# First stage in eight conditioning groups of two feature tiles instead of four of four, and background conditioning blocks at other places

## The chip, the cores and the metric

One NeuronCore of a Trainium2 chip. The metric is the device time of one execution in microseconds. The engines are TensorE (PE), ScalarE (ACT), VectorE (DVE), GpSimd (POOL, which only issues DMAs here) and SyncE (SP, DMAs too).

## The reference

One layer of a diffusion backbone: 512 latent tokens and 256 context tokens of 2048 features, all in float32. What matters here:

```python
sh1, sc1, gt1, sh2, sc2, gt2 = modulation(c, w_ada, b_ada)          # silu(c) @ w_ada + b_ada, 2048 -> 12288
csh1, csc1, ...              = modulation(c_ctx, w_ada, b_ada)      # only shift and scale 1 are used
hc = modulate(rms_norm(ctx, g_mix_pre), csh1, csc1)                 # h * (1 + scale) + shift
hx = modulate(rms_norm(x,   g_mix_pre), sh1,  sc1)
u_f, u_x, u_g = split(h @ w_in)    # Fourier group, RG-LRU input, RG-LRU gate branch; 1024 features each
# x_c = conv(u_x); bidirectional RG-LRU on ctx, then on x; times gelu(u_g); Fourier mix of u_f
x = x + gt1 * rms_norm(concat(...) @ w_out, g_mix_post)
x = x + gt2 * rms_norm(conv_ffn(modulate(rms_norm(x, g_ffn_pre), sh2, sc2)), g_ffn_post)
```

## The kernel before, in words

Features lie on the partitions: x is 16 feature tiles of 128 x 512, ctx 16 of 128 x 256. Every float32 product is three matmuls (`three`, L679 on): a rounded high part and a low part of weights and of activations, hi*hi, hi*lo, lo*hi. The weights come as a stream of units of 128 x 1024 (eight 128 x 128 blocks, 512 KB) through a ring of five slots. SP loads unit n when unit n - 5 has been used (`load_unit`), ACT rounds it (`hi`, L377), DVE takes the difference (`lo`, L1013), and PE uses the blocks. Each engine runs a list of instructions whose order is written out by hand, with semaphores between them.

**The conditioning.** `w_ada` has 12288 columns. The first 4096 (shift and scale 1) are needed before anything can be projected. They are computed on PE in the first stage, for c and c_ctx at once: `ada_unit` (L694) multiplies a loaded unit of 128 x 1024 (one row tile k, 512 columns of shift and 512 of scale) by the two columns of csil, into two of the four 32-column strips of the array, so that units of even and odd k run beside each other. After 16 units a group of four feature tiles has its sums as rows in bank 5; ACT copies them (`copy_rows`, L406), and PE turns them into columns in bank 7 (`turn`, L706, with `pick`, which also adds the strips up).

**The first stage** (L688 to L750). PE adds up the squares of x and of ctx with ones-matmuls. Then, for each of four groups: DVE's `modulate` (L1101) makes gains, scales the tiles of x and ctx, ACT's `round_h` (L412) makes the high parts, DVE the low parts (L1121, L1123), and PE's `first_heads(k)` (L721) multiplies tile k with the weights of heads 0 and 1: the gate branch (u_g) and the input (u_x, also for ctx). The units of the next group go between the tiles. All sums of heads 0 and 1 are complete only with tile 15, since the tiles are summed over k.

**The heads.** For h in 0 to 7 PE projects head h + 2 and computes the recurrence gates of head h; ACT does the seeds of the convolution (`seeds`), gelu, sigmoids, exponentials and roots; DVE convolves, combines and scans (`convolve`, `gap`, `finish_head`). In heads 6 and 7 PE turns to the Fourier projections.

**The Fourier stage** (four groups: weights_dft, channel_mix, token_dft), with halves of the output projection between, then **the output projection**: tiles 4 to 15 each take two weight units, and DVE adds the square of each tile (`add_square`), splits the weights of the tile after the next, adds positions to the residual (`place`), and eats background blocks. Then the norms, and the feed-forward part.

**The background blocks.** The other 8192 columns of `w_ada` are 8 sums of 16 blocks each, 128 x 1024, 512 KB. POOL loads them into three slots (`load_ada`, L333): block q is loaded when q - 2 are eaten. DVE eats a block (`eat_ada`, L1034): acc = acc + block * csil, one instruction of 128 x 1024. After 16 blocks PE sums acc over the partitions (`sum_ada`, L759: 8 matmuls of one column), and DVE reads the result (`take_ada`, L1056). There are two accumulators; a sum's first block waits until the sum that had its accumulator is done (`ADA_FREE`). How many blocks each head eats is in `ADA_SLOT`, after which output tile a sum is made in `SUM_AFTER`, and in which round of DVE it is taken in `TAKE_AT`. Before the output projection 32 blocks have been eaten, in it 64, in the feed-forward part 32.

Of the kernel before, what the change touches and what calls it, by code (L numbers as in the profile page):

```python
# [13 lines left out]
P = 128  # L14
# [18 lines left out]
UX, UG = {0: (1, 7), 1: (1, 7)}, {0: (0, 6), 1: (0, 6)}  # L33
# [31 lines left out]
NADA = 4  # L65
# [3 lines left out]
NBG = (6 * D - NADA * 1024) // ACOL  # L69
FFN_ADA = NBG - 2  # L70
ADA_SLOT = (4, 3, 3, 3, 3, 0, 3, 3)
ADA_FREE = (0, 1, 0, 2, 3, 4, 6, 7)
SUM_AFTER = {4: 1, 6: 2, 9: 3, 12: 4, 15: 5}
TAKE_AT = {5: 1, 7: 2, 10: 3, 13: 4}
# [35 lines left out]
def build(nc, x_t, ctx_t, par_d, late_d, stream, ada0, adabg, gates_d, tabs_d, wf_d, out_t):  # L110
    ctx = ExitStack()
    with ctx:
# [44 lines left out]
        with ExitStack() as s:  # L157
            c0, hc_lo = twice(s, "c0", "hc_lo", [P, KT, C])
            hc_hi = sbuf(s, "hc_hi", [P, KT, C], F32R)
            with ExitStack() as s0:  # L160
                sq0 = sbuf(s0, "sq0", [P, 2, L])
                ss_x = sbuf(s0, "ss_x", [P, L])
                ss_c = sbuf(s0, "ss_c", [P, C])
                pos0 = sbuf(s0, "pos0", [P, NPOS])
                ada_rows = sbuf(s0, "ada_rows", [P, 512])
                ada0_raw = sbuf(s0, "ada0_raw", [P, A0SLOTS, 1024])
# [56 lines left out]
        def ada_acc(n):  # L223
            return (ada_acc1 if n in (2, 4) else ada_acc0)[:, :]
# [4 lines left out]
        x_in, c_in = [sem(f"x_in{i}") for i in range(4)], sem("c_in")  # L229
# [11 lines left out]
        h_pre, h_rounded, h_ready = sem("h_pre"), sem("h_rounded"), sem("h_ready")  # L241
        gates_done, xc_seed, xc_done, xc_round, xc_split = (
# [48 lines left out]
        def _(sp):  # L291
# [12 lines left out]
            for i in range(4):  # L304
                sp.dma_start(x0[:, 4 * i:4 * i + 4, :], x_t[:, 4 * i:4 * i + 4, :]).then_inc(x_in[i], 16)
                load_a0(i)
            for i in range(2):
                sp.dma_start(c0[:, 8 * i:8 * i + 8, :], ctx_t[:, 8 * i:8 * i + 8, :]).then_inc(c_in, 16)
# [22 lines left out]
        def _(pool):  # L331
# [23 lines left out]
            load_ada(19, 25)  # L355
# [4 lines left out]
            load_ada(25, 30)  # L360
            load_wf(2)
            load_ada(30, 32)
            load_wf(3)
            load_ada(32, 34)
            pool.wait_ge(yc_ready, KT)
            pool.dma_start(late_par[:, :], late_d).then_inc(late_in, 16)
            for j in range(4):
                pool.dma_start(x1[:, 4 * j:4 * j + 4, :], x_t[:, 4 * j:4 * j + 4, :]).then_inc(x1_in[j], 16)
                load_ada(34 + 8 * j, 42 + 8 * j)
            load_ada(66, NBG * KT)  # L370

        @block.scalar
        def _(act):
# [24 lines left out]
            act.wait_ge(c_in, 32)  # L398
            for k in range(KT):
                square(sq0[:, k % 2, 0:C], c0[:, k, :], KT + k)  # L400
            act.wait_ge(csil_done, 2)
            act.wait_ge(sq_added, 2 * KT)
            std(bank[0], ss_x[:, :])
            std(bank[1], ss_c[:, :])

            def copy_rows(c):  # L406
                act.wait_ge(a0_used, KT * c + KT)
                if c > 0:
                    act.wait_ge(turned, c)
                a.activation(ada_rows[:, :], bank[5][:, :], ACT.Copy).then_inc(rows_copied, 1)  # L410

            def round_h(c):  # L412
                for k in range(4 * c, 4 * c + 4):
# [5 lines left out]
            hi(0, 1)  # L419
            copy_rows(0)  # L420
            round_h(0)
            hi(2, 3)
            copy_rows(1)
            round_h(1)
            hi(4)
            copy_rows(2)
            round_h(2)
            hi(5)
            copy_rows(3)
            hi(6, 7)  # L430
            round_h(3)
            hi(8, 9)

            def gelu(h):
                act.wait_ge(*used(UG[h][1]))
# [46 lines left out]

            seeds(0)
            hi(10, 11)
            gelu(0)
            gelu(1)
# [189 lines left out]
        def _(pe):  # L676
# [17 lines left out]
            def ada_unit(u):  # L694

                k, s = u % KT, u % A0SLOTS
                pe.wait_ge(a0_in[s], 16 * (u // A0SLOTS) + 16)
                if k == 0 and u > 0:
                    pe.wait_ge(rows_copied, u // KT)
                for part in range(2):  # L700
                    g = 32 * (2 * (k % 2) + part)
                    mm = t.matmul(bank[5][g:g + 2, :], csil[:, 2 * k:2 * k + 2], ada0_raw[:, s, 512 * part:512 * part + 512],  # L702
                                  start=k < 2, stop=k >= KT - 2, tile_position=(0, g))
                mm.then_inc(a0_used, 1)

            def turn(c):  # L706
# [3 lines left out]
                for j in range(4):  # L710
# [3 lines left out]
            for k in range(KT):  # L714
                ada_unit(k)
                pe.wait_ge(sq_done, KT + k + 1)
                mm = t.matmul(bank[1][:, 0:C], ones, sq0[:, k % 2, 0:C], start=k == 0, stop=k == KT - 1)
                mm.then_inc(sq_added, 1)
            pe.wait_ge(std_done, 2)

            def first_heads(k):  # L721

                c, j = k // 4, k % 4
                g_unit, x_unit = 2 * c, 2 * c + 1
                pe.wait_ge(h_ready, k + 1)
                if j == 0:
                    pe.wait_ge(lo_done, g_unit + 1)
                for h in range(2):
                    mm = three(bank[UG_BANK[h]][:, :], *block_of(g_unit, 4 * h + j), h_hi[:, k, :], h_lo[:, k, :], k == 0, k == KT - 1)
                if j == 3:  # L730
                    mm.then_inc(unit_used, 1)
                if j == 0:
                    pe.wait_ge(lo_done, x_unit + 1)
                for h in range(2):
                    bx, bc = ux_bank(h)
                    w, w_l = block_of(x_unit, 4 * h + j)
                    three(bx[:, :], w, w_l, h_hi[:, k, :], h_lo[:, k, :], k == 0, k == KT - 1)
                    mm = three(bc[:, 0:C], w, w_l, hc_hi[:, k, :], hc_lo[:, k, :], k == 0, k == KT - 1)
                if j == 3:
                    mm.then_inc(unit_used, 1)  # L740

            for c in range(NADA):
                for j in range(4):
                    if c + 1 < NADA:
                        for u in range(KT * (c + 1) + 4 * j, KT * (c + 1) + 4 * j + 4):
                            ada_unit(u)
                    if j == 0:
                        turn(c)
                    first_heads(4 * c + j)
# [9 lines left out]
            def sum_ada(n, b):  # L759
# [805 lines left out]
```

## Time and profile before

| | us |
|---|---|
| median of 3 runs (lowest, highest) | 2279.06 (2275.04, 2281.58) |
| the profiled execution | 2278.63 |
| its span | 2276.8 |
| busy: PE, DVE, ACT | 2146.7, 1219.5, 715.8 |
| mean granted clock of PE | 0.969 |

The profile is one execution. The page gives the busy share of each engine in 40 slices of the span (57 us each) in tenths, and the clock that PE was granted. A list of waits says how long an engine stood and what ended it. A timeline lists instructions in order of time, with the idle time ahead of them in brackets. A window row gives the busy time of each engine in a stretch. Matmul durations include the way through the array, so the distance between starts is what a matmul costs in a row of them.

### The profile page before, as it was taken

How to read it: one execution, taken by the hardware profiler on the slowest of the kernel's cores; microseconds unless marked ns; L12 is line 12 of the kernel's file. 1: busy time of each engine (PE TensorE's matmuls, PEld its weight loads, DVE VectorE, ACT ScalarE, POOL GpSimd, SP SyncE). 2: the span in 40 equal slices, each digit the busy share in tenths (PEclk: the TensorE clock that was granted, in tenths of full speed). 3: DMA queues.
4: the chain of work that ended last, by engine and by line, in shares of the span. 5: the costliest groups of instructions: out<-in, count | busy, mean ns of one | idle time of the engine just before them, and what ended most of it. 6: DMA issues, size and time to landing. Idle time of an engine off the chain costs nothing.

```text
span 2276.8 us, 23135 instructions
## 1 busy us (share of the span) xinstructions
PE 2146.7 (94%) x9668; PEld 1725.2 (76%) x9668; DVE 1219.5 (54%) x1491; ACT 715.8 (31%) x926; POOL 74.8 (3%) x145
## 2 busy tenths in 40 slices
PE   7779999999788699999999999999999999999994
PEld 2457888888667388888888888888888888888883
DVE  2545887885666865454454544434344443434447
ACT  3224667543122333222222322222232222222222
POOL 0000000010211000000000000000000000000000
PEclk9889999999888799999999999999999999999997
DMA  9743433343777134343333432232232322232321
GB/s 387 271 182 111 130 114 114 132 159 111 285 251 260 44 133 136 119 140 102 122 128 129 133 108 93 93 100 95 93 102 93 95 100 93 94 100 93 97 98 74
DMA packets 83192, 302.39 MB, mean 133 GB/s; under 512 B 9296, under 2 KB 9424, under 8 KB 81808
## 3 DMA queue, kind: packets, MB, share of 16 engines
q1 hardware_dynamic: 63360, 227.03, 29.1%
q0 software_dynamic: 19728, 73.89, 9.7%
q8 instruction: 76, 1.25, 0.2%
q14 instruction: 28, 0.23, 0.0%
HBM read 296.69 MB, written 4.19 MB: 132 GB/s over the span
## 4 chain that ended last, share of the span: by engine, by line
PE 69%; DVE 7%; DMA 3%; ACT 1%; issue 1%; DVEq 0%; ACTq 0%
PE bank L681 23%; PE bank L683 23%; PE bank L682 23%; DMA ada_raw<-in_adabg 2%; DVE ada_acc L1053 2%; DVE w_lo L1017 1%; PE bank L762 1%; DVE x L1379 0%; DVE x L1452 0%; DVE acc L1377 0%; DVE acc L1450 0%; DVE ss L1029 0%; ACT w_hi L380 0%; DMA w_raw<-in_stream 0%; DVE x L1356 0%
## 5 line engine op out<-in xcount | busy, mean ns | idle before, releaser
L681 PE MATMUL bank<-h_hi,w_hi 128*128 128x512 f32 x2048 | 809.4, 395 | 34.6 <-DVE hc_lo L1123 15.9
L682 PE MATMUL bank<-h_lo,w_hi 128*128 128x512 f32 x2048 | 804.9, 393 | 0.0
L683 PE MATMUL bank<-h_hi,w_lo 128*128 128x512 f32 x2048 | 803.4, 392 | 0.0
L1017 DVE TENSOR_TENSOR w_lo<-w_raw,w_hi 128x1024 fp32r<-128x1024 f32 x344 | 411.3, 1222 | 636.5 <-ACT w_hi L380 636.3
L380 ACT ACTIVATE w_hi<-w_raw 128x1024 fp32r<-128x1024 f32 x344 | 353.0, 1056 | 1097.3 <-PE bank L683 1034.5
L681 PEld LDWEIGHTS bank<-h_hi,w_hi 128*128 128x128 f32 x2048 | 389.5, 190 | 120.4 <-DVE hc_lo L1123 16.3
L683 PEld LDWEIGHTS bank<-h_hi,w_lo 128*128 128x128 f32 x2048 | 388.9, 190 | 82.8
L682 PEld LDWEIGHTS bank<-h_lo,w_hi 128*128 128x128 f32 x2048 | 389.7, 190 | 75.5
L683 PE MATMUL bank<-act_hi,w_lo 128*128 128x512 f32 x704 | 278.1, 395 | 0.0
L681 PE MATMUL bank<-act_hi,w_hi 128*128 128x512 f32 x704 | 278.0, 395 | 0.0
L682 PE MATMUL bank<-act_lo,w_hi 128*128 128x512 f32 x704 | 278.0, 395 | 0.0
L1427 DVE TENSOR_TENSOR acc<-acc,bank 128x512 f32<-128x512 f32 x160 | 109.1, 687 | 173.9 <-PE bank L683 173.9
L1053 DVE SCALAR_TENSOR_TENSOR ada_acc<-ada_raw,csil,ada_acc 128x1024 f32<-128x1024 f32 x120 | 153.8, 1281 | 45.2 <-DMA ada_raw<-in_adabg 40.8
L682 PEld LDWEIGHTS bank<-act_lo,w_hi 128*128 128x128 f32 x704 | 132.1, 188 | 32.1
L683 PEld LDWEIGHTS bank<-act_hi,w_lo 128*128 128x128 f32 x704 | 132.1, 188 | 32.1
L681 PEld LDWEIGHTS bank<-act_hi,w_hi 128*128 128x128 f32 x704 | 132.1, 188 | 32.0
L342 POOL DMA_DIRECT2D ada_raw<-in_adabg x128 | 67.7, 529 | 1191.4 <-DVE ada_acc L1053 803.1
L604 ACT ACTIVATE acc<-bank 128x512 f32<-128x512 f32 x16 | 9.5, 596 | 147.1 <-PE bank L683 147.1
L762 PE MATMUL bank<-par,ada_acc 128*128 128x1 f32 x128 | 21.4, 297 | 35.8 <-DVE ada_acc L1053 35.8
L762 PEld LDWEIGHTS bank<-par,ada_acc 128*128 128x128 f32 x128 | 21.4, 258 | 37.7 <-DVE ada_acc L1053 37.5
L702 PE MATMUL bank<-ada_raw,csil 128*2 128x512 f32 x256 | 41.7, 634 | 4.9 <-ACT ada_rows L410 4.9
L682 PE MATMUL bank<-hc_lo,w_hi 128*128 128x256 f32 x128 | 36.5, 285 | 0.0
(188 smaller groups left out, 1468.3 us busy)
## 6 DMA issues: line engine op xcount, KB each, us to landing
w_raw<-in_stream SPq DMA_DIRECT2D x344, 512.0 KB, 3.5
ada_raw<-in_adabg POOLq DMA_DIRECT2D x128, 512.0 KB, 4.6
ada_raw<-in_ada SPq DMA_DIRECT2D x64, 512.0 KB, 7.0
x<-in_x_t SPq DMA_DIRECT2D x4, 1024.0 KB, 12.2
x<-in_x_t POOLq DMA_DIRECT2D x4, 1024.0 KB, 6.9
out_t<-x SPq DMA_DIRECT2D x16, 256.0 KB, 2.0
c<-in_ctx_t SPq DMA_DIRECT2D x2, 1024.0 KB, 18.7
g_raw<-in_gates SPq DMA_DIRECT2D x8, 256.0 KB, 4.2
```

Source lines behind the costliest of these rows:

```text
L342: pool.dma_start(ada_raw(s), adabg[q]).then_inc(ada_in[s], 16)
L380: a.activation(w_hi[:, n % RING, :], w_raw[:, n % RING, :], ACT.Copy).then_inc(hi_done, 1)
L604: a.activation(tile(acc, m), b[:, :], ACT.Copy).then_inc(y_copied, 1)
L681: t.matmul(out, w, v, start=start, stop=False)
L682: t.matmul(out, w, v_l, start=False, stop=False)
L683: return t.matmul(out, w_l, v, start=False, stop=stop)
L702: mm = t.matmul(bank[5][g:g + 2, :], csil[:, 2 * k:2 * k + 2], ada0_raw[:, s, 512 * part:512 * part + 512], start=k < 2, stop=k >= KT - 2, ...
L762: mm = t.matmul(b[:, j:j + 1], ada_acc(n)[:, P * j:P * j + P], ones[:, 0:1], start=True, stop=True)
L1017: v.tensor_tensor(w_lo[:, s, :], w_raw[:, s, :], w_hi[:, s, :].bitcast(F32), ALU.subtract).then_inc(lo_done, 1)
L1053: v.scalar_tensor_tensor(dst, ada_raw(s), scale, dst, ALU.mult, ALU.add).then_inc(ada_eaten, 1)
L1427: v.tensor_tensor(tile(acc, m), tile(acc, m), bank[4 + m % 4][:, :], ALU.add).then_inc(down_added, 1)
```

## The change

- The first 4096 columns come in eight groups of two feature tiles (NADA 8). A unit now holds two row tiles k and, of each, 256 columns of shift and 256 of scale; 8 units make a group, 64 in all as before. `ada_unit` issues four matmuls of 256 columns into the four strips.
- SP loads x and ctx ahead of all conditioning units, and weight unit c behind the fourth unit of group c. Weight units 0 to 7 each hold the gate and the input weights of heads 0 and 1 for two tiles.
- PE adds up the squares of ctx first, then runs the 8 units of group 0. ACT makes the root for x after the fourth square of ctx.
- In each group PE runs the first unit of the next group, the turn, four more units, gates of tile 2c, inputs, two units, gates and inputs of tile 2c + 1, the last unit. In the last group both gates come ahead of the inputs, and ACT's gelu of heads 0 and 1 waits for the gates alone (`first_ug`), ahead of its seeds.
- Background blocks: heads eat 28 instead of 22, the Fourier stage 12 instead of 10, the output projection 56 instead of 64. The sum of blocks 0 to 15 is made in head 4 (bank 4), that of 16 to 31 in `channel_mix(2)` (bank 6, columns 8 to 15), the sums 2 to 5 after output tiles 6, 9, 13 and 15.

```diff
-ADA_SLOT = (4, 3, 3, 3, 3, 0, 3, 3)
-SUM_AFTER = {4: 1, 6: 2, 9: 3, 12: 4, 15: 5}
+ADA_SLOT = (4, 4, 4, 4, 0, 4, 4, 4)
+SUM_AFTER = {6: 2, 9: 3, 13: 4, 15: 5}
@@ sync
-                load_a0(i)
...
-            for u in range(4, NADA * KT):
+            for u in range(NADA * A0UNITS):
                 load_a0(u)
-                at = {8: (0, 1), 24: (2, 3), 30: (4,), 46: (5,), 60: (6, 7)}
-                for n in at.get(u, ()):
-                    load_unit(n)
+                if u % A0UNITS == 3:
+                    load_unit(u // A0UNITS)
@@ scalar
             for k in range(KT):
+                if k % 8 == 0:
+                    act.wait_ge(c_in[k // 8], 16)
                 square(sq0[:, k % 2, 0:C], c0[:, k, :], KT + k)
+                if k == 3:
+                    std(bank[0], ss_x[:, :])
...
+            hi(0)
+            for c in range(NADA):
+                copy_rows(c)
+                round_h(c)
+                hi(c + 1)
...
+            gelu(0)
+            gelu(1)
+            hi(9)
             seeds(0)
             hi(10, 11)
-            gelu(0)
-            gelu(1)
@@ tensor
+                for q in range(4):
+                    k, g = 2 * i + q // 2, 32 * q
+                    mm = t.matmul(bank[5][g:g + 2, 0:2 * P], csil[:, 2 * k:2 * k + 2], ada0_raw[:, slot, 256 * q:256 * q + 256],
+                                  start=i == 0, stop=i == A0UNITS - 1, tile_position=(0, g))
...
             for c in range(NADA):
+                after = range(A0UNITS * (c + 1), A0UNITS * (c + 2)) if c + 1 < NADA else ()
+                for u in after[0:1]:
+                    ada_unit(u)
+                turn(c)
+                for u in after[1:5]:
+                    ada_unit(u)
+                pe.wait_ge(lo_done, c + 1)
+                pe.wait_ge(h_ready, 2 * c + 1)
+                gates_of_two(2 * c)
+                if c + 1 < NADA:
+                    inputs_of_two(2 * c)
+                    for u in after[5:7]:
+                        ada_unit(u)
+                    pe.wait_ge(h_ready, 2 * c + 2)
+                    gates_of_two(2 * c + 1)
+                    inputs_of_two(2 * c + 1)
+                    for u in after[7:8]:
+                        ada_unit(u)
+                else:
+                    pe.wait_ge(h_ready, 2 * c + 2)
+                    gates_of_two(2 * c + 1)
+                    inputs_of_two(2 * c)
+                    inputs_of_two(2 * c + 1)
...
                 project_gate(h + 2)
+                if h == 4:
+                    pe.wait_ge(xc_done, 6)
+                    sum_ada(0, bank[4])
                 gates(h, 1)
+                if h == 4:
+                    pe.wait_ge(ada_read, 1)
             pe.wait_ge(xc_done, 7)
-            sum_ada(0, bank[2])
...
                 mm.then_inc(nyq_done, 1)
+                if g == 2:
+                    sum_ada(1, bank[M_BANK[0]], 8)
@@ vector (Fourier stage)
-            eat_ada(3)
+            eat_ada(2)
...
-            eat_ada(2)
+            eat_ada(1)
...
             split_yc(8, 9)
-            eat_ada(2)
...
             split_yc(10, 11)
-            eat_ada(1)
+            take_ada(1, bank[M_BANK[0]], 8)
...
             fourier_input(7)
+            eat_ada(2)
             lo(56)
             fourier_output(2)
+            eat_ada(1)
             split_yc(12, 13)
             read_nyq(3)
             split_p(3)
-            eat_ada(1)
+            eat_ada(2)
             fourier_output(3)
             split_yc(14, 15)
+            eat_ada(3)
@@ vector (output projection, in round m)
                 if 3 <= m < 15:
-                    eat_ada(6 if m % 3 == 0 else 5)
+                    eat_ada(4 if m % 3 == 2 else 5)
```

## Rows read from the trace of the kernel before

**Rows 1.** The page, 40 slices: busy tenths of PE and its granted clock.

```profile
PE   7779999999788699999999999999999999999994
...
PEclk9889999999888799999999999999999999999997
```

**Rows 2.** Windows: stretch, length, busy us of PE, PEld, DVE, ACT, POOL, PEclk, DMA share, GB/s.

```profile
0.00:57.00 57.00, 42.66 (x128) 12.02 (x128) 12.52 (x24) 21.17 (x39) 0.20 (x4) 1.00 0.98 387
57.00:182.00 125.00, 97.05 (x514) 63.74 (x515) 56.25 (x97) 35.85 (x55) 1.71 (x3) 0.85 0.58 216
```

**Rows 3.** Waits of PE over the span: total us, times, longest.

```profile
PE bank L762 <- DVE ada_acc L1053: 35.8, 4, 13.4
PE bank L681 <- DVE hc_lo L1123: 15.9, 4, 4.0
...
PE bank L681 <- DVE w_lo L1017: 4.3, 2, 3.5
```

**Rows 4.** Timeline of PE, first stage: start, us, instruction, count, idle before.

```profile
12.81 17.27 PE L691 MATMUL bank<-sq,par 128*128 128x512 f32 x32 [12.81 <-ACT sq L385]
...
30.98 0.70 PE L717 MATMUL bank<-sq,par 128*128 128x256 f32 x2
...
81.43 1.90 PE L702 MATMUL bank<-ada_raw,csil 128*2 128x512 f32 x16
83.26 0.50 PE L681 MATMUL bank<-h_hi,w_hi 128*128 128x512 f32 x1
...
86.93 1.90 PE L702 MATMUL bank<-ada_raw,csil 128*2 128x512 f32 x16
...
99.28 0.80 PE L681 MATMUL bank<-h_hi,w_hi 128*128 128x512 f32 x1 [3.98 <-DVE hc_lo L1123]
...
122.75 1.05 PE L711 MATMUL bank<-par,ada_rows 128*128 128x4 f32 x8
127.78 0.80 PE L681 MATMUL bank<-h_hi,w_hi 128*128 128x512 f32 x1 [3.98 <-DVE hc_lo L1123]
...
181.33 0.80 PE L681 MATMUL bank<-h_hi,w_hi 128*128 128x512 f32 x1 [5.12 <-ACT y_lru L436]
```

**Rows 5.** Timeline of ACT: a square of ctx, a table load, a square after a root.

```profile
31.71 0.42 ACT L385 ACTIVATE sq<-c 128x256 f32<-128x256 f32 x1 [1.17 <-PE bank L717]
...
55.56 1.28 ACT L388 ACT_TABLE_LOAD   x1 [2.80 <-PE bank L717]
...
758.23 0.63 ACT L619 ACTIVATE sq<-x 128x512 f32<-128x512 f32 x1 [4.99 <-DVE x L1379]
```

**Rows 6.** Timeline of DVE: the reciprocal for x.

```profile
57.57 3.35 DVE L1029 RECIPROCAL ss_x<-ss_x 128x512 f32<-128x512 f32 x1 [31.10 <-ACT ss_x L388]
```

**Rows 7.** Timelines of DVE and PE, heads.

```profile
349.42 0.96 DVE L1158 SCALAR_TENSOR_TENSOR lru_u<-lru_r,lru_u 128x768 f32<-128x768 f32 x1 [3.14 <-ACT lru_r L465]
...
390.48 0.50 PE L681 MATMUL bank<-h_hi,w_hi 128*128 128x512 f32 x1 [1.14 <-ACT y_lru L436]
...
416.38 0.47 PE L681 MATMUL bank<-xc_hi,g_hi 128*128 128x512 f32 x1 [1.75 <-issue]
```

**Rows 8.** Timelines of PE and DVE, Fourier stage.

```profile
486.37 0.47 PE L681 MATMUL bank<-h_hi,w_hi 128*128 128x512 f32 x1 [1.57 <-DVE h_lo L1267]
...
536.01 0.61 DVE L1253 TENSOR_SCALAR eo<-bank,nyq_p 128x129 f32<-128x129 f32 x2 [0.29 <-PE bank L683]
...
539.19 0.24 PE L852 MATMUL bank<-nyq,m_hi 128*128 128x2 f32 x1 [0.47 <-DVE y_four L1259]
```

**Rows 9.** Output projection: window of ada_acc (PE, PEld, DVE), lines of DVE, PE's timeline.

```profile
566.00:747.00 181.00, 12.56 (x64) 12.41 (x64) 79.77 (x64) 0.87 0.76 264
...
L1053 DVE SCALAR_TENSOR_TENSOR ada_acc<-ada_raw,csil,ada_acc 128x1024 f32<-128x1024 f32 x60 | 77.0, 1284 | 44.0 <-DMA ada_raw<-in_adabg 40.8 <-DVE ada_acc L1053 0.5
...
L1025 DVE TENSOR_TENSOR ss<-ss,sq 128x512 f32<-128x512 f32 x13 | 8.9, 686 | 13.0 <-ACT sq L385 13.0
...
608.62 3.58 PE L762 MATMUL bank<-par,ada_acc 128*128 128x1 f32 x16 [13.36 <-DVE ada_acc L1053]
```

More of the change, by code:

```diff
@@ L694, in ada_unit @@
             def ada_unit(u):
[L696 to L703, printed above, removed]
+                i, slot = u % A0UNITS, u % A0SLOTS
+                pe.wait_ge(a0_in[slot], 16 * (u // A0SLOTS) + 16)
+                if i == 0 and u > 0:
+                    pe.wait_ge(rows_copied, u // A0UNITS)
+                for q in range(4):
+                    k, g = 2 * i + q // 2, 32 * q
+                    mm = t.matmul(bank[5][g:g + 2, 0:2 * P], csil[:, 2 * k:2 * k + 2], ada0_raw[:, slot, 256 * q:256 * q + 256],
+                                  start=i == 0, stop=i == A0UNITS - 1, tile_position=(0, g))
                 mm.then_inc(a0_used, 1)
@@ L709, in turn @@
                     pe.wait_ge(mod_made, c)
-                for j in range(4):
+                for j in range(2):
                     mm = t.matmul(bank[7][:, 4 * j:4 * j + 4], ada_rows[:, P * j:P * j + P], pick, start=True, stop=True)
@@ L718, in _, with gates_of_two @@
                 mm.then_inc(sq_added, 1)
+            for u in range(A0UNITS):
+                ada_unit(u)
             pe.wait_ge(std_done, 2)
[L721 to L727, printed above, removed]
-                for h in range(2):
[L729 to L733, printed above, removed]
+            def gates_of_two(k):
+                for h in range(2):
+                    mm = three(bank[UG_BANK[h]][:, :], *block_of(k // 2, 2 * h + k % 2), h_hi[:, k, :], h_lo[:, k, :],
+                               k == 0, k == KT - 1)
+                    if k == KT - 1:
+                        mm.then_inc(first_ug, 1)
@@ L757, in half, with sum_ada @@
                 mm.then_inc(unit_used, 1)
-            def sum_ada(n, b):
+            def sum_ada(n, b, at=0):
                 pe.wait_ge(ada_eaten, n * KT + KT)
                 for j in range(ACOL // P):
-                    mm = t.matmul(b[:, j:j + 1], ada_acc(n)[:, P * j:P * j + P], ones[:, 0:1], start=True, stop=True)
+                    mm = t.matmul(b[:, at + j:at + j + 1], ada_acc(n)[:, P * j:P * j + P], ones[:, 0:1], start=True, stop=True)
                 mm.then_inc(ada_summed, 1)
@@ L821, in _ @@
             gates(7, 0)
-            pe.wait_ge(ada_read, 1)
             project_fourier(3)
@@ L832, in weights_dft @@
                     pe.wait_ge(m_split, 2 * g)
+                    if g == 3:
+                        pe.wait_ge(ada_read, 2)
                 pe.wait_ge(wf_lo_done, g + 1)
@@ L1124, in modulate @@
                                                ALU.add, ALU.subtract).then_inc(h_ready, 1)
-            modulate(0)
-            lo(2, 3)
-            modulate(1)
-            lo(4)
-            modulate(2)
-            lo(5, 6, 7)
-            modulate(3)
-            lo(8, 9)
+            for c in range(NADA):
+                modulate(c)
+                lo(c + 1)
             def convolve(h):
@@ L1294, in _ @@
                 input_of(h, 0)
+                if h == 4:
+                    take_ada(0, bank[4])
                 lo(n0 + 6, n0 + 7)
```

113 lines of the change are left out of this document (46 added, 67 removed).

## The prediction

> **What bounds the kernel now.** I read the page's busy tenths first. TensorE (PE) is at 9 nearly everywhere, and dips in two places, each with a dip in its granted clock: the first tenth, and slices 10 to 13 [rows 1]. The windows by stage: the stretch from 57 to 182 is 97 of 125 us busy at a mean clock of 0.85 [rows 2], while the feed-forward part behind slice 14 is full and the change leaves it alone. The list of PE's waits says what it waited for [rows 3]: four waits of 3.98 us for the split activations of a group (hc_lo), 4.3 for split weights, and 35.8 us in four waits for sums of background conditioning blocks (ada_acc, L762). The last is the largest, and lies in the output projection. So two stages decide: the first, where a chain conditioning → rows → turn → modulate stands between PE and its next group, and the output projection, where VectorE (DVE) must eat 64 background blocks while 12 tiles pass.
>
> **The change part by part.**
>
> *First stage, until group 0 starts.* The kernel before needs 16 units of 512 KB for the first group, now 8, and the order on SP puts x and ctx ahead of them. DVE gets its first x piece at the same time and PE's 16 squares of x, which PE itself paces, end at 30.1 as before [rows 4]. Then the squares of ctx, which alternated with conditioning units, run alone. One costs 0.42 on ACT and 0.70 on PE [rows 4, 5], with about 0.18 of hand-over, in two buffers: 1.30 per two, so 16 end at 30.1 + 15 x 0.65 + 0.7 = 40.5. The root of x's sum now stands after ctx square 3: a table load of 1.28 and 0.69, of which 0.2 is covered: 42.3. In exchange its reciprocal (3.35 us on DVE) [rows 6] hides under the other squares; only ctx's 1.75 is left, beside the units. The 8 units: four took 1.83 between row starts (81.43 to 83.26) [rows 4], and the new ones have twice the matmuls at half the columns in all four column strips, so I take the same 0.46 each: 46.0. If a matmul of 256 columns cost as much as one of 512, a unit would be 0.92; that is the upper bound, the lower is 0.43. Then 0.8 for the copy of 256 columns with its waits, 0.5 for the next unit, 0.6 for a turn of half the size (8 records took 1.06), and the 3.98 from turn to PE: group 0 starts at 51.9. It started at 69.8 before: 17.9 us earlier.
>
> A rule of the Trainium skill speaks against the moved root: "ScalarE: Activation LUTs", section on table sets, says that calls are to be batched by set, since each change of set loads a table. Here the row of 758.23 shows Square after Sqrt without a load between [rows 5], so the trace doesn't bear it out for this pair; by the rule a second pair of loads would add 2.6 us at the 1.28 of the row.
>
> *One group of two tiles, of which there are now eight.* A tile's 18 matmuls took 3.67 us with the change-over (83.26 to 86.93) [rows 4]; two of them and the change-overs 7.3; units 5 and 6 0.95; from unit 7 to the next group's first unit 1.25, because the copy (0.42 + two hand-overs) is no longer covered by a tile; that unit 0.5; turn 0.6; 3.98 of modulation, under which four units (1.8) now run, so PE is idle for about 2.1. Sum 14.6 us for two tiles. Before, four tiles took 28.5 from start to start (99.28 to 127.78), so the groups themselves gain almost nothing: they pay the modulation latency twice as often and hide half of it. What they do take away is the late weight unit (the 3.5 us wait for w_lo) [rows 3] and the half-speed stretch behind it, since a unit of weights now comes every eight units. Group 7 starts at 51.9 + 7 x 14.6 = 154.1. The transfers (64 conditioning units, 8 of weights, x and ctx, about 44 MB; at the 387 GB/s of the first 57 us [rows 2] 114 us) stay ahead of that; the 12 slots hold SP back, not PE.
>
> *Its end.* Gates first: 2 x 1.38, then the inputs 4 x 1.04: 6.9 us, to 161.0. ACT's gelu (a table load and 0.55 each) needs the gates only and is over before that, so the wait of 5.1 us for y_lru at 181.33 and the slow matmuls behind it (0.43 instead of 0.23 a piece for 3.1 us, a loss of 1.55) go [rows 4]. What is late next is nothing on PE: seeds, convolution and xc's split need 9 us, and project_gate(2) lasts 11. I add 1 us for the clock falling in one or two groups: 162.0 against 181.33 + 1.55. **First stage -21** (between -8, if every group runs slow once, and -26).
>
> *Heads.* Six more blocks are eaten here, 1.28 us each, at most two more in one head. PE is full until 390 and DVE waits 3.14 us for ACT's exponentials and more in each head (349.42) [rows 7], which covers one block a head; the split that PE needs is not late. The new waits (xc_done 6 and ada_read 1 around gates(4, 1)) end before PE comes to them, DVE's take_ada waits about 5 us for PE, with only lo(30), lo(31) behind it, which PE needs 16 us later. But the sum of block 0 (1.7 us of PE) moves out from in front of project_fourier(0): there it was covered, since PE then waited 1.14 for gelu(7) anyway [rows 7], a time set by ACT from gates(5, 1) on. In head 4 it is not: **+1.7** (0 to +3).
>
> *Fourier stage.* Two blocks fewer ahead of split_yc bring h_lo 2.6 us forward and take away the wait of 1.57 at 486.37. The sum of block 1 comes to channel_mix(2) from the output projection: +1.7 on PE here, nothing saved there, because DVE bounds that stage. eat_ada(2) now stands ahead of fourier_output(2), which began 0.3 us after its PE input; PE waits for it already 0.47 us (539.19) [rows 8]: +1.95. **+2.1** (-2 to +5). Bank 6 and the new wait ada_read 2 cost nothing: take_ada stands where DVE has waited for PE.
>
> *Output projection.* In the 181 us from 566 to 747 DVE eats 64 blocks, 79.8 us of work; it waits 40.8 for their transfers and 13.0 for squares (tiles 7, 10 and 13, each just after PE stood at a sum) [rows 9]. A tile takes PE 11 us, a round of DVE 12 to 15, so DVE with its three slots is the bound, and PE stands only at the sums. After the change 56 blocks are eaten: 8 x 1.28 = 10.2. Those dropped are the last of their rounds, beyond the three slots that are full: with them go about 6 us of the transfer waits. The sums of blocks 2 to 4 now stand where their blocks have been eaten for a tile (after tiles 6, 9, 13: 48, 64, 80 eaten in rounds 4, 7, 11), so PE runs ahead and the 13 us for squares go. That is 29; as 4.2 MB less moves in 15% less time, I give back 2 to 3 for slower transfers. The sum of block 5 still waits for the last round. **-27** (-12 to -35; PE's own 12 x 11 + 5 us is the floor).
>
> Sum: 2276.8 - 21 + 1.7 + 2.1 - 27 = 2232.6 of span, with the 1.8 around it 2234.4; the profiled execution (2278.63) is 0.4 below the median shown, so **2235**.
>
> **The rivals.**
> *The clock falls in every group.* All stalls of 4 us ended in half speed (behind 99.28, 127.78 and 181.33) [rows 4]; one such stretch of 3.2 us, a matmul at 0.43 instead of 0.23, costs 1.6. For it: each group has an idle of 2.1 and one of 0.7 with only thin conditioning matmuls between. Against it: at 416.38 an idle of 1.75 cost no clock [rows 7]. 8 x 1.6, less the 1 counted: 2247. The Trainium skill has the rule that speaks for it ("TensorE: Matmul & The Clock Gate", section on depth-cycling): frequent short idles between groups of matmuls already bring throttling and rewarming. The trace has no such series, so it can't decide.
> *The output projection is bound by transfers, not by slots.* If the rate stays at 264 GB/s [rows 9], 4.2 MB less saves 16 us, not 27: 2246. Against it: the engines moved 387 in the first 57 us [rows 2].
> *Slower than before: the clock never comes back in the first stage.* At half speed a group is tiles 14.2, units 1.9, 1.7 and 1.0, turn 1.0, modulation 4.0: 23.8. Seven times 9.2 and 7 more at the end, less 1: +70, 2305. It decides from 5.4 us a group. For it: half of a group is thin matmuls and holes. Against: 7 us of dense matmuls in each group, where after 99.28 and 181.33 some 3 us of them brought it back [rows 4].
> *The start is later than I walk it* is in the range: each 0.46 on a unit is 13 to 17 us.
>
> **How the numbers follow.** The forecast, 2226 to 2243: 0.50. Clock in every group 0.18; transfers bound 0.15; both, 2258: 0.05; better than 2226, 0.06; slower 0.04; something between 2258 and 2280 that I don't see 0.02. The range of 8 in 10 takes in the first two rivals: 2222 to 2256. A difference under 0.3% (7 us) can't be told from none: faster 0.94, same 0.02, slower 0.04.
>
> **What would show it.** PE's first group at 52, then every 14.6, project_gate(2) at 162 without a wait; in PE's list hc_lo eight times at about 2 us, no y_lru of 5; the sums' waits (35.8) down to one of a few us; 154 us instead of 181 from round 3 to 15, with waits for w_lo in their place; a wait near 2 us ahead of the last channel_mix, and one of 2.8 for gelu(7). I am wrong if units cost 0.9, if the granted clock is under 0.9 between 52 and 160, or if DVE's waits for ada_raw stay near 40.

## The result, and the profile after

The changed kernel takes 2249.43 us (median of 4 runs, 2240.91 to 2252.67), the kernel before on the same chip 2279.57: a ratio of 0.9865, 95% interval 0.9834 to 0.9896. Four more runs of the same file beside the experiments gave 2247.51, ratio 0.9867 [0.9853, 0.9880] (brackets hold the 95% interval, here and below). So it is faster by some 30 us. I had forecast 2235, with a range of 2222 to 2256; the forecast band itself, 2226 to 2243, was missed by 6 us.

The profiled execution is the fastest of the four: 2240.91, its span 2239.1 against 2276.8 before, 37.7 less. The other three had a mean granted clock of 0.976, this one 0.980. That is 9 us in the sum (0.004 of 2240), and I come back to it.

The page, 40 slices, busy tenths and granted clock of PE, to be laid beside [rows 1]:

```profile
PE   6789999999897899999999999999999999999994
...
PEclk9989999999998999999999999999999999999997
```

Counted from 1, the clock was at 8 in slices 2 and 3, and at 8, 8, 8 and 7 in slices 11 to 14; it is at 8 in slices 3 and 13 alone. PE's own tenths in slices 11 to 14 went from 7, 8, 8, 6 to 8, 9, 7, 8. By windows, beside [rows 2]:

```profile
0.00:55.00 55.00, 37.99 (x189) 17.41 (x190) 24.77 (x40) 26.42 (x47) 0.20 (x4) 0.97 0.85 330
55.00:162.00 107.00, 85.15 (x680) 57.32 (x679) 41.46 (x91) 25.86 (x43) 1.70 (x3) 0.93 0.75 285
545.00:720.00 175.00, 151.73 (x664) 123.87 (x662) 124.67 (x116) 44.04 (x60) 32.53 (x62) 0.93 0.79 282
```

PE is busy for 80% of the second window and not 78%, at a clock of 0.93 and not 0.85, and the stage is shorter. The waits of PE, beside [rows 3]:

```profile
PE bank L679 <- DVE hc_lo L1142: 20.0, 8, 4.1
...
PE bank L679 <- DVE w_lo L1036: 11.2, 5, 3.9
...
PE bank L774 <- DVE ada_acc L1072: 8.2, 1, 8.2
```

The four waits for sums (35.8) are now one of 8.2, at the last sum (5). All five waits for weights (11.2) lie in the output projection, where the kernel before had 0.8, so they took up 10 of what the sums left. The wait for y_lru of 5 is gone. And hc_lo comes eight times: seven times 2.2 to 2.6, once 4.1. PE's timeline of the first stage, beside [rows 4]:

```profile
33.97 8.30 PE L714 MATMUL bank<-sq,par 128*128 128x256 f32 x24 [1.60 <-ACT sq L386]
42.20 3.63 PE L700 MATMUL bank<-ada_raw,csil 128*2 128x256 f32 x64
46.42 0.61 PE L700 MATMUL bank<-ada_raw,csil 128*2 128x256 f32 x8 [0.59 <-ACT ada_rows L413]
...
51.63 0.47 PE L679 MATMUL bank<-h_hi,w_hi 128*128 128x512 f32 x1 [2.22 <-DVE hc_lo L1142]
...
66.32 0.47 PE L679 MATMUL bank<-h_hi,w_hi 128*128 128x512 f32 x1 [2.22 <-DVE hc_lo L1142]
...
81.41 0.47 PE L679 MATMUL bank<-h_hi,w_hi 128*128 128x512 f32 x1 [2.63 <-DVE hc_lo L1142]
...
82.22 0.63 PE L679 MATMUL bank<-h_hi,w_hi 128*128 128x512 f32 x1
...
85.94 0.40 PE L681 MATMUL bank<-h_hi,w_lo 128*128 128x512 f32 x1
...
97.68 0.47 PE L679 MATMUL bank<-h_hi,w_hi 128*128 128x512 f32 x1 [2.22 <-DVE hc_lo L1142]
...
158.97 0.76 PE L679 MATMUL bank<-h_hi,w_hi 128*128 128x512 f32 x1 [4.06 <-DVE hc_lo L1142]
...
163.37 0.63 PE L680 MATMUL bank<-h_lo,w_hi 128*128 128x512 f32 x1
...
168.33 0.40 PE L679 MATMUL bank<-h_hi,w_hi 128*128 128x512 f32 x1
...
179.23 0.39 PE L679 MATMUL bank<-xc_hi,g_hi 128*128 128x512 f32 x1
```

Read the starts of the groups first: 51.63, 66.32, 81.41, 97.68, then (not shown) 112.38, 128.66, 144.92, and 158.97. The distances are 14.69, 15.09, 16.27, 14.70, 16.28, 16.26 and 14.05. Apart from the 15.09, behind which stands a longer hole (2.63), a full group is either some 14.7 or 16.3. What the 1.6 are is seen inside the third group: its matmuls start 0.42 apart at 82.22 (0.63 long) and 0.23 apart at 85.94 (0.40 long). Those are the two levels of the clock, 1.2 and 2.4 GHz. Its first matmul, at 81.41, was still fast; the clock fell a moment behind the hole. In the last group the clock is down at its first matmul. project_gate(2) has 48 matmuls of 512 columns, and the first gate matmul of head 0 follows them at 179.23, so project_gate(2) begins at 168.33.

The Fourier stage and the output projection, timelines of PE and DVE, beside [rows 8, 9]; the squares at L1044 mark the rounds, of which 552.94 is round 3 and 710.53 round 15:

```profile
529.26 0.24 PE L869 MATMUL bank<-nyq,m_hi 128*128 128x2 f32 x1 [1.86 <-DVE y_four L1273]
...
710.67 3.57 PE L774 MATMUL bank<-par,ada_acc 128*128 128x1 f32 x16 [8.24 <-DVE ada_acc L1072]
```

```profile
547.22 0.42 DVE L1041 COPY ss<-sq 128x512 f32<-128x512 f32 x1
...
552.94 0.69 DVE L1044 TENSOR_TENSOR ss<-ss,sq 128x512 f32<-128x512 f32 x1
...
710.53 0.69 DVE L1044 TENSOR_TENSOR ss<-ss,sq 128x512 f32<-128x512 f32 x1
```

The same three squares of the kernel before:

```profile
556.85 0.43 DVE L1022 COPY ss<-sq 128x512 f32<-128x512 f32 x1 [3.58 <-ACT sq L385]
...
565.80 0.69 DVE L1025 TENSOR_TENSOR ss<-ss,sq 128x512 f32<-128x512 f32 x1
...
747.15 0.68 DVE L1025 TENSOR_TENSOR ss<-ss,sq 128x512 f32<-128x512 f32 x1
```

So the 37.7 us of the two profiled executions are: first stage 181.33 + 1.55 - 168.33 = 14.6 gained; from there to the first square 373.97 before, 378.89 now, 4.9 lost; from the first square to round 15 190.30 before, 163.31 now, 27.0 gained; and 1.1 behind it.

### The profile page after: what moved, and what is told of

It reads as the page before. It is cut to its first block, busy times and chain, and to the rows that moved or that the text cites. A ratio compares the mean times of both kernels' runs of the same rounds, so it can differ in the third digit from the quotient of the medians.

```text
span 2239.1 us, 23688 instructions
## 1 busy us (share of the span) xinstructions
PE 2127.7 (95%) x9924; PEld 1722.9 (77%) x9924; DVE 1220.5 (55%) x1507; ACT 716.4 (32%) x930; POOL 74.8 (3%) x145
## 4 chain that ended last, share of the span: by engine, by line
PE 73%; DVE 6%; DMA 3%; issue 1%; ACT 1%; DVEq 0%; ACTq 0%
PE bank L679 24%; PE bank L680 24%; PE bank L681 24%; DMA ada_raw<-in_adabg 3%; DVE w_lo L1036 1%; DVE ada_acc L1072 1%; DVE x L1395 0%; DVE x L1468 0%; DVE acc L1466 0%; DVE acc L1393 0%; DMA w_raw<-in_stream 0%; DVE ss L1048 0%; PE bank L774 0%; DVE x L1372 0%; PE bank L869 0%
## 5 line engine op out<-in xcount | busy, mean ns | idle before, releaser
L1072 DVE SCALAR_TENSOR_TENSOR ada_acc<-ada_raw,csil,ada_acc 128x1024 f32<-128x1024 f32 x120 | 153.8, 1281 | 41.0 <-DMA ada_raw<-in_adabg 36.7
L700 PE MATMUL bank<-ada_raw,csil 128*2 128x256 f32 x512 | 32.9, 379 | 4.2 <-ACT ada_rows L413 4.2
L681 PE MATMUL bank<-hc_hi,w_lo 128*128 128x256 f32 x128 | 36.4, 284 | 0.0
```

Source lines behind the costliest of these rows:

```text
L681: return t.matmul(out, w_l, v, start=False, stop=stop)
L700: mm = t.matmul(bank[5][g:g + 2, 0:2 * P], csil[:, 2 * k:2 * k + 2], ada0_raw[:, slot, 256 * q:256 * q + 256], start=i == 0, stop=i == A0U ...
L1072: v.scalar_tensor_tensor(dst, ada_raw(s), scale, dst, ALU.mult, ALU.add).then_inc(ada_eaten, 1)
```

## The experiments

They were run in three sets, each on one chip of its own and with the kernel before beside it, whose median was 2277.34, 2277.69 and 2277.90. The changed kernel itself was run again in the first set only, with the new first stage alone, the background blocks alone and the filled holes. Where another kernel is compared with its 2247.51, the two ran on different chips. My theory after the result was this: the two parts of the change work as forecast, and the first stage fell short because the granted clock falls behind its holes. The rival: something in the stage other than the clock, or a part that costs more than I think.

**The changed kernel again**, as the level for the others.

> The changed kernel once more, nothing edited. Theory (clock): its executions differ by how many groups of the first stage and tiles of the output projection fall into half speed; the execution that was profiled (2240.9, mean granted clock 0.980) had few of them, those at 2249 to 2253 (0.976) had some five stretches of 3.4 us more. Expected: median 2249 (2245 to 2253), and a profile with groups that last 16.2 us instead of 14.7 in a number that goes with its time, 1.6 us each. Rival (transfers): the spread comes from DMA latency, the groups all last the same and the waits for ada_raw and w_raw carry the difference.

Measured: 2247.51 (2243.83 to 2249.58), ratio 0.9867. Its profile (2243.83) has three long groups again, but not the same ones (the third, fourth and sixth; before the third, fifth and sixth): 14.71, 15.07, 16.27, 16.24, 14.70, 16.26, 14.07. So which groups lose the clock can differ from one execution to the next. It mostly doesn't: the traces of four kernels below (the new first stage alone, the old end, the block eaten later, the early sums) start their groups in the same way and lose it in the third, fourth and sixth too. It is three of the first seven in all six traces.

**The new first stage alone**: its order and the last group's end as after, all background blocks as before.

```diff
-SUM_AFTER = {6: 2, 9: 3, 13: 4, 15: 5}
+SUM_AFTER = {4: 1, 6: 2, 9: 3, 12: 4, 15: 5}
...
-                    eat_ada(4 if m % 3 == 2 else 5)
+                    eat_ada(6 if m % 3 == 0 else 5)
```

> The new first stage alone; the background blocks, their sums and their takes as before the change. Theory (the two parts are independent and add up): first stage 12 to 14 us shorter up to project_gate(2), everything behind as before: 2279.6 - 13 = 2266 (2260 to 2271), PE's waits at the sums again about 36 us. Rival (the gain of the first stage is given back later, since DVE or the transfers are behind): 2275 or more.

Measured: 2261.39 (2259.85 to 2265.81), ratio 0.9932 [0.9920, 0.9945]: 16 below before. PE's four waits for sums are still there (34.9).

**The background blocks alone**, with the first stage of before.

```diff
-SUM_AFTER = {4: 1, 6: 2, 9: 3, 12: 4, 15: 5}
+SUM_AFTER = {6: 2, 9: 3, 13: 4, 15: 5}
...
-                    eat_ada(6 if m % 3 == 0 else 5)
+                    eat_ada(4 if m % 3 == 2 else 5)
```

> The moved background blocks and sums alone, on the first stage of the kernel before. Theory: output projection 24 to 27 us shorter, heads and Fourier stage 1 to 4 us longer: 2279.6 - 24 = 2256 (2251 to 2260), so that this part is the larger of the two. Rival (heads pay for the blocks): DVE with 28 blocks in the heads gets late, PE waits for xc_split or w_lo there, 2265 or more.

Measured: 2258.57 (2257.54 to 2260.78), ratio 0.9918 [0.9905, 0.9932]: 19 below before. Its first square stands at 562.59 and round 15 at 726.17, 163.58 us, close to the changed kernel's 163.31. So this half of the change gives its 27 whatever the first stage does. The two parts alone add to 34.7 and together give 29.8; each ratio is known to some 3 us, so this is no proof that they hinder each other.

**The holes filled.** Matmuls with weights of zero, added into the open sum of bank 1, where PE would wait: five (of two passes, as float32) ahead of each group but the first, nine ahead of the last, one while the rows are copied.

```diff
+            def fill(n):
+
+                for _ in range(n):
+                    t.matmul(bank[1][:, 0:256], zeros[:, :], par[:, 0:256], start=False, stop=False)
...
                 for u in after[1:5]:
                     ada_unit(u)
+                fill(0 if c == 0 else 5 if c + 1 < NADA else 9)
```

> The changed kernel, with matmuls of zero weights (128 x 128 by 256 columns, 0.43 us each, added to an open sum, so they change nothing) in the holes of the first stage: one behind the last unit of each group, five ahead of the wait for h_ready in groups 1 to 6, nine in group 7. They take the idle time of PE, not its work. Theory (clock): no group falls to half speed, each lasts 14.7, group 7 has no half-speed gates, project_gate(2) starts at 162 to 163 instead of 169, median 2238 to 2242, 8 to 11 less than the changed kernel. Rival (PE's clock is not what makes groups last 16.2, the transfers or DVE are): groups stay at 14.7 to 16.3, median within 3 of the changed kernel, or above it where a fill comes in the way of real work.

Measured: 2237.07 (2232.68 to 2240.77), ratio 0.9822 [0.9807, 0.9837], 10.4 below the changed kernel on the same chip, though PE does more work and the chain from a turn to the next group is no shorter. Its PE timeline (L708 is the filler):

```profile
51.65 0.77 PE L680 MATMUL bank<-h_hi,w_hi 128*128 128x512 f32 x1 [2.21 <-DVE hc_lo L1151]
...
95.06 2.42 PE L708 MATMUL bank<-par,zeros 128*128 128x256 f32 x10
97.34 0.47 PE L680 MATMUL bank<-h_hi,w_hi 128*128 128x512 f32 x1
...
141.44 0.47 PE L680 MATMUL bank<-h_hi,w_hi 128*128 128x512 f32 x1
...
155.48 0.47 PE L680 MATMUL bank<-h_hi,w_hi 128*128 128x512 f32 x1
```

The only group with a hole left, the first, is the only slow one (0.77 for its first matmul), though the same hole cost nothing in the six traces without filler. From 97.34 to 141.44 are three groups of 14.7, the two ahead of them (not shown) also take 14.7, and the last begins at 155.48 and at full speed. So what made groups last 16.3 was the clock. By the rows this is worth 6.4 us: the first gate matmul of head 0 stands at 173.38, and at 179.75 in the changed kernel run again (0.5 of it lies ahead of group 0). Where the other 4 of the 10.4 between the medians lie, the traces don't show.

**The sums later, alone**, in the kernel before.

```diff
-SUM_AFTER = {4: 1, 6: 2, 9: 3, 12: 4, 15: 5}
-TAKE_AT = {5: 1, 7: 2, 10: 3, 13: 4}
+SUM_AFTER = {4: 1, 7: 2, 10: 3, 13: 4, 15: 5}
+TAKE_AT = {5: 1, 8: 2, 11: 3, 14: 4}
```

> The kernel before with the sums of blocks 2 to 5 behind tiles 6, 9, 12 and 15 as before against one tile later: here behind 7, 10, 13 and 15. Nothing else differs, and 64 blocks are still eaten in the output projection. My theory: the gain of the output projection has two parts, fewer blocks and sums that no longer wait. The sums alone take away PE's stands at tiles 7, 10 and 13 and with them DVE's waits for squares (13.0 us of the rows): 2264, between 2261 and 2268; PE's waits for ada_acc fall from 35.8 to the last sum's 8 to 15. Rival: DVE's rounds bound the stage whatever PE does, and then the later sums give nothing: 2277.

Measured: 2269.30 (2266.11 to 2273.21), ratio 0.9960 [0.9947, 0.9974], 8.4 below before: between the two expectations. Waits of PE over the span, and of DVE in the output projection:

```profile
PE bank L681 <- DVE w_lo L1017: 20.9, 7, 4.7
...
PE bank L762 <- DVE ada_acc L1053: 12.1, 2, 9.3
```

```profile
DVE ada_acc L1053 <- DMA ada_raw<-in_adabg: 46.3, 25, 3.9
...
DVE ss L1025 <- ACT sq L385: 0.7, 1, 0.7
```

DVE's waits for squares are gone, as I expected. But 5.5 us of them come back as waits for transfers (40.8 to 46.3), and PE now waits for w_lo where it waited for sums. With 64 blocks DVE's rounds, waits for transfers included, set the pace again as soon as the sums don't.

**The old end of the last group** in the changed kernel: inputs before gates, gelu behind the seeds.

```diff
-                if c + 1 < NADA:
+                if True:
                     inputs_of_two(2 * c)
...
-            gelu(0)
-            gelu(1)
             hi(9)
             seeds(0)
             hi(10, 11)
+            gelu(0)
+            gelu(1)
```

> The changed kernel with the last group's end in its old order: inputs before gates, and gelu behind the seeds. My theory: the wait for y_lru comes back ahead of the first gate projection (5 us with something off, since the group has two tiles and not four: 2 to 5) and the matmuls behind it run at half speed for 3 us (1.6): 3 to 7 us above the changed kernel, 2251 to 2255. Rival: the clock is already at half speed in the last group, so nothing is lost there, or the seeds and the convolution take what is gained: 2248, no difference.

Measured: 2250.34 (2250.03 to 2257.32), ratio 0.9887 [0.9873, 0.9900], 2.8 above the changed kernel, and the two intervals overlap. In PE's timeline the step is plain:

```profile
173.38 0.80 PE L679 MATMUL bank<-h_hi,w_hi 128*128 128x512 f32 x1 [5.12 <-ACT y_lru L433]
173.97 0.63 PE L680 MATMUL bank<-h_lo,w_hi 128*128 128x512 f32 x1
```

project_gate(2) starts 4.5 later than in the changed kernel run again (168.85), and nine slow matmuls behind it lose 0.2 each: 6.5 by the rows, about as far as the profiled executions of the two lie apart (2250.03 and 2243.83). The medians show less than half of it.

**One block eaten later**: `eat_ada(2)` behind fourier_output(2).

```diff
             fourier_input(7)
-            eat_ada(2)
             lo(56)
             fourier_output(2)
-            eat_ada(1)
+            eat_ada(3)
```

> The changed kernel with the block that stands ahead of fourier_output(2) eaten behind it. My theory: it is on VectorE's path to TensorE's next input, the 1.9 us wait for y_four goes: 2 us below the changed kernel, 2245 to 2246. Rival: the block only moves the wait to the last fourier_output or to the first sum: no difference, 2248.

Measured: 2241.14 (2239.45 to 2246.15), ratio 0.9843 [0.9829, 0.9856]. 6 below where 2 were expected. The wait for y_four fell from 1.86 to 0.47, and from project_gate(2) to the first square the trace takes 377.57 us where the changed kernel's takes 378.89: 1.3 gained. The 6 of the medians is not in the profiled executions: behind the first square this one is slower, 166.53 us to round 15 against 163.31 and 164.36 in the two of the changed kernel. That points to the rival, the wait moves on. The pair at the end gives 3 by its medians.

**The first stage pipelined by one group.** The rows and the turn of group c + 1 stand between the two tiles of group c, so DVE modulates the next tiles while PE works, and all eight units of the group after that stand behind the second tile.

```diff
+            turn(0)
+            units(1, 0, 8)
             for c in range(NADA):
...
-                for u in after[0:1]:
-                    ada_unit(u)
-                turn(c)
-                for u in after[1:5]:
-                    ada_unit(u)
                 pe.wait_ge(lo_done, c + 1)
                 pe.wait_ge(h_ready, 2 * c + 1)
                 gates_of_two(2 * c)
                 if c + 1 < NADA:
                     inputs_of_two(2 * c)
-                    for u in after[5:7]:
-                        ada_unit(u)
+                    turn(c + 1)
                     pe.wait_ge(h_ready, 2 * c + 2)
                     gates_of_two(2 * c + 1)
                     inputs_of_two(2 * c + 1)
-                    for u in after[7:8]:
-                        ada_unit(u)
+                    units(c + 2, 0, 8)
```

> The changed kernel with its first stage pipelined by one group: the rows and the turn of the next group are made while a group's two tiles are on TensorE, so that the modulation on VectorE lies beside matmuls, and the group after that has its eight units behind the tiles. My theory: the hole in front of each group (2.2 to 2.6 us, seven times, and 4.1 in the last) and the fall of the clock behind it go, and a group is bound by TensorE's 7.3 + 8 x 0.46 + turn and copy 1.5 = 12.5 us, or by its 4.7 MB at 387 GB/s (12.2): the stage ends 15 to 25 us earlier, 2223 to 2233. The wait for hc_lo is below 5 us in sum. Rival: the units need transfers that the 12 slots cannot bring so early, or VectorE's casts and modulations (for both tiles) bound the group at 14.5: the holes come back as waits for w_lo or ada_raw, and the gain is only the clock, 10 us: 2237 to 2240.

Measured: 2212.78 (2207.48 to 2217.14), ratio 0.9713 [0.9699, 0.9728], 34.7 below the changed kernel, more than I expected. Windows of the first stage, with one of the kernel before under them, and PE's timeline:

```profile
50.00:75.00 25.00, 23.55 (x217) 15.96 (x218) 13.77 (x29) 7.43 (x14) 0.00 (x0) 1.00 1.03 411
75.00:100.00 25.00, 24.66 (x217) 17.38 (x218) 11.84 (x26) 7.40 (x13) 0.00 (x0) 1.00 1.03 408
```

```profile
25.00:50.00 25.00, 25.00 (x87) 6.28 (x86) 1.27 (x9) 8.44 (x19) 0.00 (x0) 1.00 1.03 409
```

```profile
51.03 0.50 PE L679 MATMUL bank<-h_hi,w_hi 128*128 128x512 f32 x1
...
62.53 0.50 PE L679 MATMUL bank<-h_hi,w_hi 128*128 128x512 f32 x1
...
74.85 0.50 PE L679 MATMUL bank<-h_hi,w_hi 128*128 128x512 f32 x1
...
129.09 0.47 PE L679 MATMUL bank<-h_hi,w_hi 128*128 128x512 f32 x1 [0.48 <-DVE hc_lo L1142]
...
136.07 0.40 PE L679 MATMUL bank<-h_hi,w_hi 128*128 128x512 f32 x1
```

A group lasts 11.5 to 12.3 us where I had 12.5, the last full one, which has no units behind it, 8.1. The clock is 1.00 throughout, and project_gate(2) starts at 136.07, 32.3 earlier than at 168.33. Of these 32.3 the waits for hc_lo are 19.5 (20.0 before, 0.5 left), those for the rows 3.6 (4.2, 0.6 left), and the slow stretches 7.1. In the windows PE is busy for 94 and 99% and the share of the 16 DMA engines is 1.03: both are near full use. PE waits for a block once a group, 0.2 to 0.8, and 2.7 us in all. The transfers run at 411 GB/s where I had counted 387 from the rows. That was too low from the start, since 387 is a mean over 57 us: the kernel before moved 409 between 25 and 50.

**The sums early**, in the changed kernel: each right behind the round in which its last block is eaten.

```diff
-SUM_AFTER = {6: 2, 9: 3, 13: 4, 15: 5}
-TAKE_AT = {7: 2, 10: 3, 14: 4}
+SUM_AFTER = {4: 2, 7: 3, 11: 4, 15: 5}
+TAKE_AT = {5: 2, 8: 3, 12: 4}
```

> The changed kernel with the sums of blocks 2, 3 and 4 behind tiles 4, 7 and 11, in whose rounds their last background block is eaten, and not behind 6, 9 and 13. Still 56 blocks in the output projection. Theory A, by the prediction: TensorE stands at each sum until the block is eaten, cannot run ahead, and VectorE then waits for squares; the waits for ada_acc go from 8 to some 30 us and the time by 8 to 15: 2256 to 2263. Theory B, from the run with later sums alone (8.4 us where 13 to 16 were expected): VectorE's rounds bound the stage, most of the 27 us came from the eight blocks fewer, and early sums cost under 5 us: 2248 to 2253, with waits for ada_acc in the place of waits for w_lo.

Measured: 2288.58 (2282.38 to 2299.67, 8 runs), ratio 1.0050 [1.0031, 1.0068]: 41 above the changed kernel, and slower than the kernel before. Both expectations fell. A's mechanism is there, at three times its size; waits of PE and of DVE from 540 to 770, and PE's first early sum:

```profile
PE bank L774 <- DVE ada_acc L1072: 56.0, 4, 19.6
```

```profile
DVE ss L1044 <- ACT sq L386: 46.5, 5, 18.0
DVE ada_acc L1072 <- DMA ada_raw<-in_adabg: 31.9, 20, 3.0
```

```profile
576.95 3.58 PE L774 MATMUL bank<-par,ada_acc 128*128 128x1 f32 x16 [18.17 <-DVE ada_acc L1072]
```

PE stands 14 to 20 us for a round of DVE. Then DVE's next round needs a square of a tile that PE has not made yet, and stands 13 to 18 us itself. At each early sum the two take turns and don't overlap, and the slow matmuls behind each stall come on top (the sum at 576.95 takes 3.58; one of the kernel before, at 571.52 and without a stall ahead of it, took 1.84).

**The pipelined stage and the later block together**, beside the pipelined one again.

> The pipelined first stage once more, on the same chip as the next kernel, for the comparison with it: 2213, within 3 us.

> The pipelined first stage together with the block that is eaten behind fourier_output(2). The two lie in stages apart, and nothing in between lets time of the one be lost in the other: 2 us below the pipelined kernel if the block is worth its wait of 1.9 us alone, 6 below if the gain of the single run of it (6 us, more than its wait) was its own; nothing if that gain was the spread between sets of runs: 2207 to 2213.

Measured: 2213.29 (2212.00 to 2214.86), ratio 0.9717 [0.9704, 0.9729], and 2210.24 (2205.59 to 2211.93), ratio 0.9699 [0.9685, 0.9712]. The medians lie 3 apart and the intervals overlap. The wait ahead of channel_mix(3) is again 0.47 for 1.86. But as above the profiled execution loses in the output projection what it gains there (166.42 us from the first square to round 15, against 160.82 and 161.79 in the two pipelined ones), and at 2211.93 it is no faster than theirs (2207.48, 2212.00). So 1.3 us of the block's gain are seen in the rows, and why the medians show 3 and 6 stays open. At 2210 this is the best version of the study: 68 below the kernel before, 37 below the changed one.

## Why the prediction was right, and where not

*The start of group 0.* Forecast 51.9, measured 51.63. Eight units of 256 columns took 3.63 us, 0.45 each against the 0.46 taken; the bound of 0.92 was far off. The moved root stands in the rows as PE's wait of 1.60 at 33.97, where I had charged 1.8; the squares end at 42.20 for 42.3.

*The groups.* This is the term that was too small. I had 14.6 a group and 1 us in all for a clock that falls "in one or two groups". Where it stayed, a group took 14.69 and 14.70, once 15.09. It fell in three of seven, 1.6 each: group 7 at 158.97 and not 154.1. It also fell at the last group, whose first twelve matmuls of 512 columns ran at 0.43 (2.4 us). Of the 6.3 us by which project_gate(2) came late (168.33 for 162.0), the first three falls are 4.7, and that of the last group is 1.4 beyond the 1 us counted. Its dense part takes 6.95 at full speed, where I had 6.9. First stage: -14.6 for -21.

*The last group's hole.* I gave every group the idle of 2.1 because units fill the rest of the 3.98. Behind the last turn there are no units left, so the hole is 4.06. That costs no time in the sum (the units are missing too: 14.05), but the clock fell behind it in all six traces with this hole, as behind every stall of 4 us in [rows 4].

*From profile to median.* The profiled execution was 8.5 below the median, and the mean clock of the other runs is 0.004 lower: 9 us. With the holes filled the clock is 0.980 to 0.983 in all five runs and the median 10.4 lower. It is tempting to say that in most executions more groups fall than in the profiled one, but the traces speak against it: all six have three falls in the first seven groups, and from the start of group 0 to project_gate(2) the five with the new end take 116.7 us each. What does vary between traces is the output projection. From round 3 to round 15 the changed kernel takes 157.6 us in one and 159.2 in the other, and the kernel with the block eaten later 161.7. Whether that is where the other executions lose their 8.5 isn't shown, since they have no trace.

*The rival at 2247.* I had given 0.18 to a clock that falls in every group. The median of 2247 to 2249 is nearer to it than to the forecast, but partly by luck: the groups' falls come to 4.7 + 2.4 = 7.1 us, where that rival has 12.8, and the rest of the way to the median is the open part above. What misled me was the row that I set against it: one hole of 1.75 with dense matmuls on both sides [rows 7] kept the clock. Here the hole of 2.2 and one of 0.6 have only thin conditioning matmuls between them. Other rows agree with that difference: a hole of 2.43 between dense matmuls kept the clock (615.86, the changed kernel run again), one of 2.14 right behind a sum's thin matmuls lost it (587.59, the changed kernel). No run varies the thin matmuls alone. The rule of the Trainium skill that I had set beside that rival ("TensorE: Matmul & The Clock Gate", on depth-cycling) agrees with this series, with 14.7 and 16.3 us for the same work.

*Heads and Fourier stage.* Forecast +3.8, measured +4.9: up to the end of the wait for gelu(7) +1.8 for +1.7, behind it +3.1 for +2.1. The wait ahead of channel_mix(3)'s first matmul was forecast at 2, and is 1.86. The 2.8 for gelu(7) is there as 1.76 of issue at 374.25 and 1.13 of y_lru at 377.71.

*Output projection.* Forecast -27, measured -27.0 from the first square, but the stretch that I had forecast, rounds 3 to 15, gave 23.8 of it (157.6 for 154) and 3.2 came ahead of it. The parts are roughly right: DVE's waits for squares went from 13.0 to 1.2, those for transfers fell from 40.8 to 36.7 and not by 6. I had named waits that stay near 40 as a sign of being wrong. They nearly did, and the stage gained all the same. Later sums alone gave 8.9 from the first square to round 15 (181.40 in that kernel), so the blocks are worth some 18 where they come together (I had 10.2 + 6), and the sums less than 13. The two can't be priced apart: in the kernel before, making the sums one tile later is worth 8, and in the changed one making them two tiles earlier costs 41. The rival that transfers bound the stage is out: the rate rose from 264 to 282 GB/s as the stage got shorter.

*What I hadn't seen* is that the stage's own order was the larger prize. I had read the latency of modulation as the price of small groups. The pipelined kernel puts that latency beside a tile's matmuls. Whether the old groups of four tiles, started one group ahead, would have gained as much was not run.

## What to carry to other kernels

Where an engine waits for a chain of its own making (sums, rows, modulation, split), try to start the chain one group ahead: here the smaller groups with the new end gave 16 us, and the same groups with the chain one group ahead 35 more. (Large groups with the chain ahead were not run.) Add to each hole in front of TensorE what the slow matmuls behind it cost (here 1.6 us behind one of 2.2 to 2.6, in three cases of seven, and 2.4 us behind one of 4.1). When an engine of one pipeline consumes a sum that another makes in rounds, leave it two tiles of room. With one, in the kernel before, TensorE stood 8 to 13 us at each of three sums; with two, at most 2.7 us at such a sum; right behind the last round, 14 to 20 us, and the two take turns.

## What the runs showed of the hardware

The granted clock fell behind holes of 2.2 us in some groups and not in others of the same execution, with the same instructions around them. In all six traces with these holes it was three of the first seven groups, nearly always the same three (the third, fourth and sixth in five of the six). Behind each hole of 4 us in the first stage it fell. Matmuls on zero weights in those holes held it (0.98 from 50 to 160 us, against 0.94), and the kernel was 10.4 us shorter by its median. The DMA engines moved 409 to 412 GB/s over 25 us at a share of 1.03, in the kernel before (25 to 50), in the changed one (50 to 75) and in the pipelined one.
